# Hybrid S5 and retention layer on one core: first norm applied before the transposes and rounded out of PSUM, weight tiles issued ahead of the large parameters, table instructions re-cut

## The reference

```python
z = rmsnorm(h, norm_mix)                        # x * rsqrt(mean(x*x) + 1e-6) * norm_mix
u, q, k, v, g, gate_a, gate_b = split(z @ w_in) # 512 | 512 | 512 | 1024 | 1024 | 1024 | 1024
y_a = s5_branch(u, lam_re, lam_im, b_re, b_im, c_re, c_im, d_skip, log_step, w_glu, b_glu)
y_b = retention_branch(q, k, v, g)
merged = sigmoid(gate_a) * (y_a @ w_proj_ssm) + sigmoid(gate_b) * (y_b @ w_proj_ret)
h = h + merged @ w_out
h = h + square(relu(rmsnorm(h, norm_mlp) @ w_up)) @ w_down
out = rmsnorm(h, norm_final)
```

```python
step = exp(log_step)
mag  = exp(lam_re * step)
a_r, a_i = mag * cos(lam_im * step), mag * sin(lam_im * step)
k = (a - 1) / lam                               # complex
bb = k * b                                      # complex, 16 channels for each state
state[t] = a * state[t-1] + bb @ u[t]
y[t] = Re(c @ state[t]) + d_skip * u[t]
```

## Time and profile before

| what | us |
|---|---|
| median of three runs | 1684.61 (1683.6 to 1693.4) |
| the profiled execution | 1681.67 |
| its span, first to last instruction | 1679.6 |
| PE busy in the span | 1565.9 (93%) |
| DVE, POOL, ACT busy | 767.8, 471.0, 294.2 |
| mean granted TensorE clock, as a share of full speed | 0.974 |

### The profile page before, as it was taken

How to read it: one execution, slowest core, us unless ns; L and a number is a source line. 1 busy time by engine, 2 the same in 40 slices (tenths; PEclk the granted TensorE clock), 3 DMA queues, 4 the chain that set the end, 5 groups by cost and what they waited for, 6 DMA issues and landing times.

```text
span 1679.6 us, 20842 instructions
## 1 busy us (share of the span) xinstructions
PE 1565.9 (93%) x7608; PEld 1309.8 (78%) x7608; DVE 767.8 (46%) x1636; ACT 294.2 (18%) x591; POOL 471.0 (28%) x267
## 2 busy tenths in 40 slices
PE   5696999999999998897998999999999999999996
PEld 4475787878888787785887878888888888888885
DVE  4898646562463636356633742222222222222225
ACT  5110111220222222122100520101010100101012
POOL 1313123234131313303333023323241415060601
PEclk9798999999999999898999999999999999999998
DMA  5232334345110101101552011112020203030202
GB/s 139 75 118 84 106 100 128 97 149 194 47 51 25 50 25 36 64 1 57 177 184 66 1 51 42 60 30 71 25 75 12 87 0 100 0 100 0 87 0 100
DMA packets 95106, 118.12 MB, mean 70 GB/s; under 512 B 25552, under 2 KB 59472, under 8 KB 95056
## 3 DMA queue, kind: packets, MB, share of 16 engines
q1 hardware_dynamic: 63312, 77.97, 15.3%
q10 hardware_dynamic: 31744, 39.48, 7.5%
HBM read 95.53 MB, written 20.97 MB: 69 GB/s over the span
## 4 chain that ended last, share of the span: by engine, by line
PE 79%; DVE 14%; SPq 3%; issue 2%; ACT 1%; ACTq 1%; DMA 0%; DVEq 0%
PE acc L479 25%; PE acc L480 25%; PE acc L481 25%; DVE rs_tmp L1230 2%; DVE coef L1295 1%; DVE tb L1515 1%; SPq L349 1%; PE aux L722 1%; PE aux L716 1%; DVE rsn L1621 1%; DVE coef L1290 1%; PE aux L725 1%; PE aux L609 1%; DVE kvk L1624 1%; ACTq L960 1%
## 5 line engine op out<-in xcount | busy, mean ns | idle before, releaser
L421 POOL CAST w_hi<-stage 128x1024 fp32r<-128x1024 f32 x130 | 145.6, 1120 | 1118.0 <-PE acc L481 1059.5
L423 POOL TENSOR_TENSOR w_lo<-stage,w_hi 128x1024 fp32r<-128x1024 f32 x130 | 320.4, 2465 | 10.4
L479 PE MATMUL acc<-z_hi,w_hi 128*128 128x512 f32 x448 | 180.7, 403 | 25.5 <-DVE z_lo L1217 15.0
L479 PE MATMUL acc<-m_hi,w_hi 128*128 128x512 f32 x512 | 199.3, 389 | 0.0
L481 PE MATMUL acc<-m_hi,w_lo 128*128 128x512 f32 x512 | 199.2, 389 | 0.0
L480 PE MATMUL acc<-m_lo,w_hi 128*128 128x512 f32 x512 | 199.2, 389 | 0.0
L479 PE MATMUL acc<-w_hi,hid_hi 128*128 128x512 f32 x512 | 199.2, 389 | 0.0
L480 PE MATMUL acc<-w_lo,hid_hi 128*128 128x512 f32 x512 | 199.2, 389 | 0.0
L481 PE MATMUL acc<-w_hi,hid_lo 128*128 128x512 f32 x512 | 199.2, 389 | 0.0
L1762 DVE TENSOR_TENSOR h_res<-h_res,acc 128x512 f32<-128x512 f32 x128 | 87.8, 687 | 229.1 <-PE acc L481 229.0
L479 PE MATMUL acc<-w_hi,z_hi 128*128 128x256 f32 (+1 forms) x512 | 191.7, 374 | 0.0
(11 more groups left out here) (207 smaller groups left out, 2300.2 us busy)
## 6 DMA issues: line engine op xcount, KB each, us to landing
stage<-in_w_up SPq DMA_DIRECT2D x32, 512.0 KB, 3.7
stage<-in_w_down SPq DMA_DIRECT2D x32, 512.0 KB, 3.3
stage<-in_w_in SPq DMA_DIRECT2D x28, 512.0 KB, 3.7
gate_dram<-gate_t ACTq DMA_DIRECT2D x32, 256.0 KB, 2.0
x_in<-in_x SPq DMA_DIRECT2D x8, 512.0 KB, 7.5
stage<-in_w_in SPq DMA_DIRECT2D x32, 128.0 KB, 2.3
stage<-in_w_in SPq DMA_DIRECT2D x16, 256.0 KB, 3.0
gb_t<-gate_dram ACTq DMA_DIRECT2D x16, 256.0 KB, 2.7
```

What stands on the lines that cost most here:

```text
L421: nc.gpsimd.tensor_copy(dst_hi, stage[:, s, :]).then_inc(hi_pool, 1)
L423: nc.gpsimd.tensor_tensor(dst_lo, stage[:, s, :], dst_hi.bitcast(F32), ALU.subtract)\
L479: nc.tensor.matmul(out, s_hi, m_hi_, start=first, stop=False)
```

## The change

- **Norm.** `norm_mix` is loaded as a row that is repeated over the partitions (128 x 1024). DVE's `norm_x` multiplies a chunk by its reciprocal root and by that row in one instruction before the transposes. `scale_x`, `norm_z` and `z_tmp` are gone; `hi_z` and `lo_z` read `aux`, and PE reuses a bank of `aux` when `lo_z` has read it. For one column, `rstd` uses TENSOR_SCALAR instructions with pointers in place of SCALAR_TENSOR_TENSOR. The hooks are one chunk each after steps 1, 2, 4 and 5.
- **Loads.** `ident` and `norm_mix` follow x chunk 1. After x come `log_step`, `lam_re`, `lam_im` for both halves under a semaphore of their own (`lam_in`), then weight tiles 2 and 3, and then b, c, `dskip`, `bglu`.
- **POOL.** Its first subtraction waits for `x_scaled` of 4, that is until `norm_x` of chunks 0 to 3 is done.
- **Table.** The same polynomials with fewer instructions and with independent instructions between the linked ones. The first exponential runs ahead of `lo_z` of chunks 4, 5; two further pieces stand before and behind `lo_z` of chunks 6, 7. The memset of `toep` and `prepare(0)` come ahead of `spin` and `decay`.

```diff
@@ sync @@
-            sp.dma_start(ident[:], t["ident"]).then_inc(const_in, 16)
-            sp.dma_start(nmix[:], t["norm_mix"].rearrange("a (k p) -> p (a k)", p=P), allow_slow_non_contiguous=True).then_inc(const_in, 16)
-            for c in range(1, NCH):
+            sp.dma_start(x_in[:, 1, :], x_rows[:, 1, :]).then_inc(x_ready[1], 16)
+            sp.dma_start(nmix[:], bass.AP(tensor=nmix_row.tensor, offset=0, ap=[[0, P], [1, D]])).then_inc(const_in, 16)
+            sp.dma_start(ident[:], t["ident"]).then_inc(ident_in, 16)
+            for c in range(2, NCH):
                 sp.dma_start(x_in[:, c, :], x_rows[:, c, :]).then_inc(x_ready[c], 16)
-                if c in (1, 3):
+                if c in (3, 4):
+                    load(c - 3, w_in[:, 2 * (c - 3):2 * (c - 3) + 2, 0:HALF])
+            for gp, rows in enumerate(halves):
                 sp.dma_start(coef[rows, 2, :], bass.AP(tensor=ls.tensor, offset=gp, ap=[[0, STATE], [2, PAIRS]]),
-                             allow_slow_non_contiguous=True).then_inc(par_in, 16)
+                             allow_slow_non_contiguous=True).then_inc(lam_in, 16)
+                for i, name in enumerate(("lam_re", "lam_im")):
+                    sp.dma_start(coef[rows, i, :], t[name][0, gp::2, :].rearrange("g p -> p g"),
+                                 allow_slow_non_contiguous=True).then_inc(lam_in, 16)
+            for i in range(2, 4):
+                load(i, w_in[:, 2 * i:2 * i + 2, 0:HALF])
+            for gp, rows in enumerate(halves):
                 for ri, name in enumerate(("b_re", "b_im")):
...
-            for i in range(2, 4):
-                load(i, w_in[:, 2 * i:2 * i + 2, 0:HALF])
@@ gpsimd @@
                 pool.wait_ge(hi_pool, n_done)
+                if quiet is not None:
+                    pool.wait_ge(x_scaled, quiet)
                 nc.gpsimd.tensor_tensor(dst_lo, stage[:, s, :], dst_hi.bitcast(F32), ALU.subtract)\
...
-                regular(LD_U + i, GR_U, i, i // 2, None)
+                regular(LD_U + i, GR_U, i, i // 2, None, quiet=4 if i == 0 else None)
@@ tensor @@
-                        pe.wait_ge(z_normed, n - 3)
+                        pe.wait_ge(lo_done, SP_Z + n - 3)
-            quad(OUT_U, GR_U % 2, KT, z_hi, z_lo, 0, LD_U + 1, hooks={1: (4, 5), 4: (6, 7)})
+            quad(OUT_U, GR_U % 2, KT, z_hi, z_lo, 0, LD_U + 1, hooks={1: (4,), 2: (5,), 4: (6,), 5: (7,)})
@@ vector @@
+            def norm_x(c):
+                V.scalar_tensor_tensor(out=x_in[:, c, :], in0=x_in[:, c, :], scalar=rs1[:, c:c + 1], in1=nmix[:],
+                                       op0=ALU.mult, op1=ALU.mult).then_inc(x_scaled, 1)
...
+            rstd_x(4, 4)
+            for c in range(4, NCH):
+                norm_x(c)
-            dve.wait_ge(par_in, 16 * 16)
...
+            dve.wait_ge(lam_in, 16 * 6)
+            ts(ex, cf("ls"), -175.0, 175.0, ALU.max, ALU.min)
...
+            lo_z(4)
+            lo_z(5)
...
+            dve.wait_ge(ct_ready, 1)
+            link(V.memset(toep[:].rearrange("p g s -> p (g s)"), 0.0))
...
             prepare(0)
+            sr, si = spin[:, 0, :], spin[:, 1, :]
+            unit(sn, cs)
...
             phases()
```

More of the change, by code:

```diff
@@ L234, in build @@
         const_in = sem("const_in")
+        ident_in = sem("ident_in")
+        lam_in = sem("lam_in")
         par_in = sem("par_in")
@@ L411, in _, with split @@
         def _(pool):
-            def split(ready, count, s, slot, u0, n_done, freed=None):
+            def split(ready, count, s, slot, u0, n_done, freed=None, quiet=None):
                 if freed is not None:
@@ L1263, in lo_z @@
                     lo_split(z_lo[:, 4 * b:4 * b + 4, c * P:(c + 1) * P],
-                             z_tmp[:, n % 4, :].rearrange("p (k s) -> p k s", k=4),
+                             aux[:, n % 4, :].rearrange("p (k s) -> p k s", k=4),
                              z_hi[:, 4 * b:4 * b + 4, c * P:(c + 1) * P])
             rstd_x(0, 1)
+            dve.wait_ge(const_in, 16)
+            norm_x(0)
             rstd_x(1, 1)
-            dve.wait_ge(const_in, 32)
-            norm_z(0)
+            norm_x(1)
             rstd_x(2, 2)
+            norm_x(2)
             lo_z(0)
-            for c in range(1, 4):
-                norm_z(c)
-                lo_z(c)
+            norm_x(3)
+            lo_z(1)
+            lo_z(2)
+            lo_z(3)
             rstd_x(4, 4)
-            dve.wait_ge(par_in, 16 * 16)
+            for c in range(4, NCH):
+                norm_x(c)
             slot_of = {"lr": 0, "li": 1, "ls": 2}
@@ L1370, in _ @@
-            lr, li = cf("lr"), cf("li")
-            step, mag, ang = cf("step"), cf("mag"), cf("ang")
-            exp(step, cf("ls"))
-            tt(ang, lr, step, ALU.mult)
-            exp(mag, ang)
[L1376 to L1379, removed]
-            lo_z(NCH - 1)
-            tt(ang, li, step, ALU.mult)
-            sn, cs = cf("sn"), cf("cs")
-            sincos(sn, cs, ang)
-            link(V.memset(pwr[:, 0, :], 1.0))
@@ new lines, in _ @@
+            stt(th, sk, -b4[3], th, ALU.mult, ALU.add)
+            V.tensor_scalar(ek1, ek1, MAGIC, None, ALU.subtract)
+            ts(sk, th, 2.0 / math.pi, MAGIC, ALU.mult, ALU.add)
+            exp_bits(0, ek1)
+            ts(sk, sk, MAGIC, None, ALU.subtract)
+            lo_z(6)
+            lo_z(7)
+            V.tensor_tensor(ek1, ek, ek1, ALU.subtract)
+            stt(th, sk, -h4[0], th, ALU.mult, ALU.add)
+            V.tensor_scalar(qf, sk, 0.25, -0.375, ALU.mult, ALU.add)
+            stt(th, sk, -h4[1], th, ALU.mult, ALU.add)
@@ new lines, in _ @@
+            V.tensor_tensor(qf, cp, sp_, ALU.subtract)
+            tt(qn, cp, sp_, ALU.add)
+            V.tensor_tensor(mag, ex, ibits[:, 1, :].bitcast(F32), ALU.mult)
+            V.tensor_tensor(qf, qf, qo, ALU.mult)
+            tt(qn, qn, qo, ALU.mult)
+            V.tensor_tensor(qf, sp_, qf, ALU.add)
+            tt(qn, cp, qn, ALU.subtract)
+            V.tensor_tensor(sn, qf, qs_, ALU.mult)
+            tt(cs, qn, qs_, ALU.mult)
+            V.memset(pwr[:, 0, :], 1.0)
+            V.memset(pwi[:, 0, :], 0.0)
```

252 lines of the change are left out of this document (110 added, 142 removed).

## The result

The changed kernel takes 1642.31 us (median of 4 runs, 1636.78 to 1646.21) beside 1684.91 for the kernel before (4 runs): a ratio of 0.974, 95% interval 0.971 to 0.976. The forecast was 1667, with a range of 1661 to 1676. The profiled execution took 1641.72 us, 40 less than that of before.

What follows compares the result with a forecast made beforehand. The prediction took PE's idle and slow time before the first `outputs` as the bound. Tile 2's 7.6, the quad's 8.1 and DVE's chain's 1.8 us gave 17.5, so 1684.61 became 1667.1, range 1661 to 1676.

Steps and rivals of the forecast that it cites:

- Tile 2: Loads: weight tile 2 lands near 41.5 us, so PE resumes at 45.0 instead of 52.6, a gain of 7.6 us.
- The second file of packets: Loads: the second `log_step` transfer, 1024 packets taking 9.7 us, ends at 38.2 us and blocks the tile's issue until then.
- The norm, worth nothing: First norm: the quad starts near 23.5 instead of 27.39 us, gaining nothing because the weight tile comes later; cover 6.7 us.
- The hold on POOL: First subtraction: it starts at 18.2 instead of 9.46 us, which costs nothing.
- Quad, second half: Chunks 4 to 7: the 6.1 us wait goes, and the quad ends at 60.9 against 76.56 us.
- `ct_ready` to the scan: DVE's chain from 85.2 us: 49.9 of work plus 11.2 of POOL collisions, scanned at 146.3 against 163.78.
- The stall: PE's wait for the first scan: moved, not removed; PE arrives at 132.4 us and waits 13.9.
- Behind that nothing changes: After the first scan, all later code: the same in both kernels, so no gain or loss allowed behind 170 us.
- the rivals of the prologue: Four prologue alternatives: no packet file 1657.4 (0.05), DVE holds PE 1673.4 (0.19), tile no earlier 1674.7 (0.12), slower 1687.3 (0.04).

## Why the prediction was wrong, step by step

- **Tile 2 (7.6 us): right.** PE resumed at 43.96, not 45.0. Undoing the order cost 7.5 of lead. The second file of packets landed at 36.6 where I had 38.2, and the tile 3.8 us behind it where I had 3.3.
- **The norm, worth nothing (cover 6.7 us): right.** The quad began at 25.06 (forecast 23.5), PE then stood 4.6 us for the tile, and all of that start was hidden. The hold on POOL: nothing, as said.
- **Quad, second half: right.** 15.1 us where I had 12.9 + 2.5 + 0.5; no wait in front of chunk 6.
- **`ct_ready` to the scan: right in the sum.** 83.67 to 145.29 is 61.6 us; I had 61.1, with 11.2 of collisions. By the rows of DVE the held instructions lost 3.0 in `prepare`, 5.8 in `phases` and 3.0 in the last turn of `spin`; I had 3.0, 5.5 and 2.7, the last of them in the scans, which in fact ran undisturbed in 2.63. The stall moved as written: 14.9 us (I had 13.9).
- **"Behind that nothing changes": wrong, and nearly the whole miss.** The profiled executions lie 40.0 us apart where I had 17.5; 1.0 of the missing 22.5 us is in the prologue (18.5 at the end of the scan's wait) and 21.6 are in the heads and the second norm. The sum without this error was tested: the change with the old form of `rstd` takes 1669 us in the median (1660 to 1679) and 1661.6 in the profile, where the forecast was 1667 and 1664. I said that "the stretch behind 170 us and all later code are the same in the two kernels". The diff doesn't say that. It edits the body of a helper, and that helper is called 32 times by `norm_o` in the heads and eight times in the second norm. I costed the edit only at its calls in the first norm, where it is hidden.
- **What a look would have given.** The line of L1230 above was there before: 126 instructions on one column, up to 2421 ns where 219 is the rule. In the profiled execution of before 18 instructions SCALAR_TENSOR_TENSOR of one column began inside one of POOL's, and all 18 were held; 12 TENSOR_SCALAR of one column did so, and none was. With PE's waits for `yb` and `zb`, 5.6 and 8.7 us, in the list of waits, the term would have been 14 us plus the slow clock behind those waits. It measured 21.6. ("Inside" is from 0.06 us behind the start of POOL's instruction to 0.3 us ahead of its end; without these margins it is 20 of 20.)
- **A range** built only from the rivals of the prologue could not hold it. None of the four was about a part of the program outside the stretch that I had chosen to look at.

## What to carry to other kernels

When a diff edits a helper, list its callers and read the minimum, median and maximum of each instruction in it over the whole trace before you say where the change ends. Here a spread of ten to one on a tiny instruction was another engine's work, and the form of the instruction decided whether it was held. When two engines collide, making one earlier moves the collision: ask each time what it will meet next, and delay the one that has slack. And look at the granted clock of a stretch before you give its gain to an edit made elsewhere.

## What the runs showed of the hardware

- Of DVE's small instructions that began inside one of POOL's (with the margins above), those with two tensors in SBUF were held until POOL's ended (18 of 18 SCALAR_TENSOR_TENSOR of 128x1 before, 16 of 16 in the change with the old form, 7 of 7 TENSOR_TENSOR of 128x16 in the change). TENSOR_SCALAR of 128x1, with pointers or numbers as scalars, never was: none of 12 before, none of 45 after. The Trainium skill, "SBUF — State Buffer", section "Who interferes with whom", says that a DVE instruction with two SBUF inputs contends with a GpSimd instruction that reads SBUF, and one with a single SBUF input outside the two-port modes doesn't. The trace agrees, and shows besides that a scalar taken by pointer from SBUF doesn't count as a second input.
- TENSOR_SCALAR of more columns was held too, though it has one tensor: 1.00 us for 128x2 and 1.05 for 128x4 in the changed kernel, and 4 of 4 of 128x16 in the kernel before, up to 2.26 us, each beginning inside one of POOL's instructions. The Trainium skill, "VectorE: DVE Perf Modes", section "Mode 2×_2P — use both read ports for one tensor" with "What auto-detection actually checks", has single-source instructions with both sides in SBUF take both ports where the outermost size that isn't 1 is even, or odd and equal on both sides. 2, 4 and 16 columns are even, and one column has no such size, which fits; no run here has an odd number above 1.
- The new form is slower where nothing interferes, 273 and 214 ns against 219 and 159, and still gained 21 us.
- TENSOR_TENSOR_SCAN was held like this too: eight of them took 8.48 us beside POOL's pair and 2.63 without.
- Two transfers of 4 KB, each 1024 packets of 4 bytes, kept a 512 KB tile away for 14.4 us; as one transfer of 128 rows of 128 bytes they did not.
- The same 147 matmuls, with the same wait of 3.03 us among them, took 20.83 us at a mean granted clock of 0.86 in one kernel and 18.17 at 1.00 in another.
